# Sixteen quads of weight blocks by Strassen's seven products in a two-layer encoder on one core

## The reference

```python
h = rms_norm(x, norm_w[0]); z = h @ w_in_ab        # 4096 x 13312
y = concat([oa, ob]) * silu(gate); x = x + y @ w_out_ab   # 4096 x 4096
h = rms_norm(x, norm_w[1]); z = h @ w_in_c         # 4096 x 10240
x = x + (oc * silu(gate)) @ w_out_c                # 4096 x 4096
return rms_norm(x, final_norm_w)
```

## Time and profile before

| | |
|---|---|
| time, median of 3 runs | 2813.53 us (2813.2 to 2815.36) |
| profiled execution | 2814.37 us, of which the span of its instructions is 2812.6 us |
| PE busy | 2797.6 us, 99% |
| DVE busy | 1687.7 us, 60% |
| ACT busy | 1347.7 us, 48% |
| mean granted clock of PE | 0.998 of full speed |

### The profile page before, as it was taken

One profiled execution on the slowest core, in us unless ns is written; L12 is line 12 of the kernel. 1 busy time (PEld: TensorE's weight loads), 2 busy tenths in 40 slices (PEclk: granted clock), 3 DMA queues, 4 the chain that ended last, 5 costly groups with the idle time before them and its releaser, 6 DMA issues.

```text
span 2812.6 us, 37759 instructions
## 1 busy us (share of the span) xinstructions
PE 2797.6 (99%) x12681; PEld 2329.4 (83%) x12681; DVE 1687.7 (60%) x2103; ACT 1347.7 (48%) x1654; POOL 16.4 (1%) x14
## 2 busy tenths in 40 slices
PE   9999999999999999999999999999999999999998
PEld 7888888888888888888888888888888888888886
DVE  7766666556556555566665556666655666665554
ACT  6455455445444444444443445555544455543333
POOL 0000000000000000000000000000000000000000
PEclk9999999999999999999999999999999999999999
DMA  9777777777767777677777767777676777676665
GB/s 334 222 210 232 225 226 221 224 217 228 234 209 215 228 220 239 189 254 254 253 240 222 223 211 218 231 233 220 221 226 204 231 227 225 216 251 218 215 209 187
DMA packets 357923, 637.17 MB, mean 227 GB/s; under 512 B 25376, under 2 KB 79136, under 8 KB 357792
## 3 DMA queue, kind: packets, MB, share of 16 engines
q1 hardware_dynamic: 343824, 593.52, 67.7%
q10 hardware_dynamic: 13968, 41.95, 4.1%
HBM read 585.56 MB, written 49.81 MB: 226 GB/s over the span
## 4 chain that ended last, share of the span: by engine, by line
PE 99%; DMA 0%; issue 0%; DVE 0%; ACT 0%; POOLq 0%; POOL 0%; SPq 0%; DVEq 0%; ACTq 0%
PE proj L1098 32%; PE proj L1099 32%; PE proj L1100 32%; PE o_ps L1099 1%; PE o_ps L1098 1%; PE sc_ps L1100 1%; PE o_ps L1100 1%; PE sc_ps L1099 1%; PE sc_ps L1098 1%; DMA raw<-in_w_in_ab 0%; DVE w_lo L757 0%; DVE x_fin L1091 0%; ACT w_hi L637 0%; POOLq L268 0%; POOL rms L598 0%
## 5 line engine op out<-in xcount | busy, mean ns | idle before, releaser
L757 DVE TENSOR_TENSOR w_lo<-raw,w_hi 128x1024 fp32r<-128x1024 f32 x990 | 1208.5, 1221 | 856.7 <-ACT w_hi L637 850.5
L637 ACT ACTIVATE w_hi<-raw 128x1024 fp32r<-128x1024 f32 x990 | 1049.6, 1060 | 1148.6 <-PE proj L1100 1087.3
L1098 PE MATMUL proj<-w_hi,h_hi 128*128 128x512 f32 x2936 | 1143.4, 389 | 2.0 <-issue 1.5
L1099 PE MATMUL proj<-w_lo,h_hi 128*128 128x512 f32 x2936 | 1142.8, 389 | 0.0
L1100 PE MATMUL proj<-w_hi,h_lo 128*128 128x512 f32 x2936 | 1142.1, 389 | 0.0
L1100 PEld LDWEIGHTS proj<-w_hi,h_lo 128*128 128x128 f32 x2936 | 551.2, 188 | 114.9
L1098 PEld LDWEIGHTS proj<-w_hi,h_hi 128*128 128x128 f32 x2936 | 551.4, 188 | 114.5 <-issue 2.4
L1099 PEld LDWEIGHTS proj<-w_lo,h_hi 128*128 128x128 f32 x2936 | 551.4, 188 | 109.9
L1098 PE MATMUL proj<-w_hi,y_hi 128*128 128x512 f32 x1024 | 398.4, 389 | 0.0
L1099 PE MATMUL proj<-w_lo,y_hi 128*128 128x512 f32 x1024 | 398.4, 389 | 0.0
L1100 PE MATMUL proj<-w_hi,y_lo 128*128 128x512 f32 x1024 | 398.3, 389 | 0.0
(11 more groups left out here) (115 smaller groups left out, 975.5 us busy)
## 6 DMA issues: line engine op xcount, KB each, us to landing
raw<-in_w_in_ab SPq DMA_DIRECT2D x414, 512.0 KB, 4.4
raw<-in_w_in_c SPq DMA_DIRECT2D x320, 512.0 KB, 4.4
raw<-in_w_out_ab SPq DMA_DIRECT2D x128, 512.0 KB, 4.5
raw<-in_w_out_c SPq DMA_DIRECT2D x128, 512.0 KB, 4.5
head_turn<-head_stage SPq DMA_DIRECT2D x256, 96.0 KB, 1.9
head_land<-head_turn ACTq DMA_DIRECT2D x64, 384.0 KB, 5.5
landing<-group_turn ACTq DMA_DIRECT2D x31, 512.0 KB, 5.5
group_turn<-q_stage SPq DMA_DIRECT2D x64, 128.0 KB, 3.2
```

What stands on the lines that cost most here:

```text
L637: nc.scalar.activation(w_hi[:, slot], raw[:, slot], ACT.Copy).then_inc(hi_ready, 1)
L757: nc.vector.tensor_tensor(w_lo[:, slot], raw[:, slot], w_hi[:, slot].bitcast(F32), ALU.subtract) \
L1098: nc.tensor.matmul(dst, hi, r_hi, start=start, stop=False)
L1099: nc.tensor.matmul(dst, hi, r_lo, start=False, stop=False)
```

## The change

A *quad* is four blocks, two of each group: `B11` and `B12` (row tiles of chunk c1, groups 0 and 1), `B21` and `B22` (chunk c2). With the four 128-token by 256-row pieces of the activations `A11`, `A12` (token tile 0), `A21`, `A22` (token tile 1) it is a 2 x 2 product. The change computes it, for 16 quads, by seven products in place of eight (Winograd's form of Strassen's): seven products of six matmuls each in place of four blocks of twelve. Eleven pairs have quads: 6, 8, 10, 14, 16 and 28 one each (at block 9 in 6, 8 and 10, else at block 11), 15, 18, 23 and 29 two each (at blocks 4 and 13), and 30 two (at 2 and 11).

For each quad DVE makes four combinations of raw weights, `mix` (B12-B11), `mix3` (B22-B12), B22-mix and B21-that, each 128 x 1024; ACT rounds seven operands in place of four and DVE subtracts seven times in place of four. Operands 0, 2, 4, 6 use the ring's four slots, and operands 1, 3, 5 two spare slots that lie in tiles that are free then. The combinations of the activations (`make_sums`, S1 to S4, split once) are made in pairs 6, 14, 17 and 28, and reused by later pairs. Three products gather in PSUM banks of their own (`m1`, `m6` and `m7`, which is the bank of `o_ps`), and after the last quad of a pair seven additions of 128 x 512 (`fold`) bring them into `proj`. Pairs with quads take all of group 0 first, so group 0 ends at block 18 or 20 (30 in the last pair), where before in x1 and x2 pairs it ended at 30. Where such pairs stood in loops of two or three rounds these are written out, except for pairs 7 to 10. The diff, cut to what follows it:

```diff
+def with_quads(first, second, end=()):
+    blocks, quads = [], {}
+    for e in first:
+        if isinstance(e, tuple):
+            c1, c2 = e
+            quads[len(blocks)] = e
+            blocks += [(0, c1), (1, c1), (1, c2), (0, c2)]
+        else:
+            blocks.append((0, e))
+    return blocks + [(1, c) for c in second] + list(end), quads
+REST1, REST2 = [0, 1, *range(4, KC // 2)], [0, 1, *range(6, KC // 2)]
+VG_QUADS = with_quads([*REST1[:9], (2, 3), *REST1[9:]], REST1)
+X1_QUADS = with_quads([*REST1[:11], (2, 3), *REST1[11:]], REST1)
+TWO_QUADS = with_quads([*REST2[:4], (2, 3), *REST2[4:9], (4, 5), *REST2[9:]], REST2)
+LAST_QUADS = with_quads([*REST2[:2], (2, 3), *REST2[2:7], (4, 5), *REST2[7:-2]], REST2[:-2],
+                        [(g, EARLY + c) for g in range(2) for c in range(LATE)])
 
 
 XT_PIECES = ((0, 1), (1, 2)) + tuple((k, k + 2) for k in range(2, KC, 2))
...
-        (3, [Pair("in_ab", qk(1), "qk", "B", "vg", batch=4), Pair("in_ab", vg(1), "vg", "qk", "qk", v=2)]),
+        (1, [Pair("in_ab", vg(0), "vg", "qk", "qk", v=1, quads=VG_QUADS, heads=16, combine=((5, "vg", 0, 2),))]),
+        (2, [Pair("in_ab", qk(1), "qk", "B", "vg", batch=4),
+             Pair("in_ab", vg(1), "vg", "qk", "qk", v=2, quads=VG_QUADS, heads=20, heads_step=4)]),
+        (1, [Pair("in_ab", qk(3), "qk", "B", "vg", batch=6)]),
+        (1, [Pair("in_ab", vg(3), "vg", "qk", "qk", v=4)]),
         (1, [Pair("out_ab", out_cols(0), "x1", "B", "vg", batch=7)]),
...
-        (1, [Pair("in_c", kvc(0), "kv", "h", "x1", x_batch=3)]),
-        (1, [Pair("in_c", c(0), "qg", "k", "kv", v=5)]),
+        (1, [Pair("out_ab", out_cols(1), "x1", "h", "x1", x_batch=0, quads=X1_QUADS, heads=32,
+                  combine=((6, "x1", 0, 2), (26, "x1", 1, 4)))]),
+        (1, [Pair("out_ab", out_cols(2), "x1", "h", "x1", x_batch=1, quads=TWO_QUADS, heads=32)]),
+        (1, [Pair("out_ab", out_cols(3), "x1", "h", "x1", x_batch=2, quads=X1_QUADS, heads=32, spare="x1_end")]),
+        (1, [Pair("in_c", kvc(0), "kv", "h", "x1", x_batch=3, combine=((15, "qg", 0, 2), (19, "qg", 1, 4)))]),
+        (1, [Pair("in_c", c(0), "qg", "k", "kv", v=5, quads=TWO_QUADS, heads=32)]),
         (3, [Pair("in_c", c(1), "qg", "C", "qg", batch=8)]),
         (1, [Pair("in_c", kvc(1), "kv", "C", "qg", batch=11)]),
-        (1, [Pair("in_c", c(4), "qg", "k", "kv", v=6)]),
+        (1, [Pair("in_c", c(4), "qg", "k", "kv", v=6, quads=TWO_QUADS, heads=48)]),
...
-        (1, [Pair("out_c", out_cols(3), "x2", "none", "x2")]),
+        (1, [Pair("out_c", out_cols(1), "x2", "none", "x2", quads=X1_QUADS, heads=64,
+                  combine=((6, "x2", 0, 2), (26, "x2", 1, 4)))]),
+        (1, [Pair("out_c", out_cols(2), "x2", "none", "x2", quads=TWO_QUADS, heads=64)]),
+        (1, [Pair("out_c", out_cols(3), "x2", "none", "x2", quads=LAST_QUADS, heads=64)]),
     ]
-    n = x = second = 0
...
-                    if isinstance(p.n, int) and p.n * NB + b < RING:
-                        pass
-                    else:
-                        sp.wait_ge(lo_ready, p.n * NB + b - RING + 1)
+                    if b >= RING and p.quad_at(b - RING) is not None and p.quad_at(b - RING)[2] < 3:
+                        k, _, part = p.quad_at(b - RING)
+                        sp.wait_ge(mixed, QUAD * (p.quad_n + k) + part + 1)
...
+            def quad_hi(p, k, start, part):
+                n = p.o + p.op[start]
+                (mix, mix3), mixes_done = mix_of[p.out], QUAD * (p.quad_n + k)
+                b11, _, b22, b21 = (raw[:, (start + r) % RING] for r in range(QUAD))
+                earlier = p.o + p.op[list(p.quads)[k - 1]] if k > 0 else None
...
+                def hi(r, source, count=1):
+                    if r % 2 == 0:
+                        act.wait_ge(block_done, slot_free_after(p, start + r // 2))
+                    elif r == 5:
+                        act.wait_ge(block_done, n + 2)
+                    elif earlier is not None:
+                        act.wait_ge(block_done, earlier + (6 if r == 1 else 4))
+                    elif r == 1:
+                        act.wait_ge(block_done, p.o)
+                        act.wait_ge(folded, p.folds)
...
+                if part == 0:
+                    raw_landed(p, start)
+                    hi(0, b11)
+                if part == 1:
+                    raw_landed(p, start + 2)
+                    hi(1, b22)
+                if part == 2:
+                    act.wait_ge(mixed, mixes_done + 1)
+                    hi(2, mix[:])
+                    act.wait_ge(mixed, mixes_done + 2)
+                    hi(3, mix3[:])
+                if part == 3:
+                    raw_landed(p, start + 3)
+                    hi(4, b21)
+                    act.wait_ge(mixed, mixes_done + 3)
+                    hi(5, mix[:])
+                    act.wait_ge(mixed, mixes_done + 4)
+                    hi(6, b21, 2)
+            def copy_m1(p, b):
+                if p.quads and b == p.last_quad + QUAD:
+                    act.wait_ge(folded, p.folds)
+                    act.wait_ge(block_done, p.o + p.op[p.last_quad] + OPS)
+                    nc.scalar.activation(folds_of(p)[0], m1[:], ACT.Copy).then_inc(m1_copied, 1)
...
+            def quad_lo(p, k, start, part):
+                n = p.o + p.op[start]
...
+                b11, b12, b22, b21 = (raw[:, (start + r) % RING] for r in range(QUAD))
+                minus = lambda dst, a, b: nc.vector.tensor_tensor(dst, a, b, ALU.subtract)
...
+                def lo(r, source, count=1):
+                    hi, dst = weights_of(p, start, r)
+                    dve.wait_ge(hi_ready, n + r + 1)
+                    minus(dst, source, hi.bitcast(F32)).then_inc(lo_ready, count)
+                if part == 0:
+                    lo(0, b11)
+                if part == 1:
+                    second = (start + 1) % RING
+                    dve.wait_ge(raw_loaded[second], 16 * (p.n * (NB // RING) + (start + 1) // RING + (second > 1)))
+                    dve.wait_ge(lo_ready, n + 1)
+                    minus(mix, b12, b11).then_inc(mixed, 1)
+                    lo(1, b22)
+                if part == 2:
+                    dve.wait_ge(mixed, mixes_done + 1)
+                    minus(mix3, b22, b12).then_inc(mixed, 1)
+                    lo(2, mix)
+                    dve.wait_ge(mixed, mixes_done + 2)
+                    dve.wait_ge(lo_ready, n + 3)
+                    minus(mix, b22, mix).then_inc(mixed, 1)
+                    lo(3, mix3)
+                if part == 3:
+                    lo(4, b21)
+                    dve.wait_ge(mixed, mixes_done + 3)
+                    dve.wait_ge(lo_ready, n + 5)
+                    minus(b21, b21, mix).then_inc(mixed, 1)
+                    lo(5, mix)
+                    dve.wait_ge(mixed, mixes_done + 4)
+                    lo(6, b21, 2)
+                    dve.wait_ge(lo_ready, n + OPS)
...
+                    hi, lo = sums_of[stage][quad]
+                    if b == at + 1:
+                        dve.wait_ge(sums_hi, p.combined + k + 1)
+                        nc.vector.tensor_tensor(lo[:], sums, hi[:].bitcast(F32), ALU.subtract).then_inc(sums_split, 1)
+                        continue
+                    rows = slice(2 * c1, 2 * c1 + 4)
+                    a_hi, a_lo = (y_hi, y_lo) if p.w in ("out_ab", "out_c") else (h_hi, h_lo)
+                    dve.wait_ge(block_done, p.o)
...
+                    a11, a12 = parts[:, 0:2, 0:P], parts[:, 2:4, 0:P]
+                    a21, a22 = parts[:, 0:2, P:SEQ], parts[:, 2:4, P:SEQ]
+                    s1, s2, s3, s4 = (sums[:, r] for r in range(4))
+                    dve.wait_ge(sums_made, done + 1)
+                    nc.vector.tensor_tensor(s3, a11, a21, ALU.subtract)
+                    nc.vector.tensor_tensor(s1, a21, a22, ALU.add).then_inc(sums_made, 1)
+                    dve.wait_ge(sums_made, done + 2)
+                    nc.vector.tensor_tensor(s2, s1, a11, ALU.subtract).then_inc(sums_made, 1)
+                    dve.wait_ge(sums_made, done + 3)
+                    nc.vector.tensor_tensor(s4, a12, s2, ALU.subtract).then_inc(sums_made, 1)
...
+                    dve.wait_ge(m1_copied, p.pair_w + 1)
+                    dve.wait_ge(block_done, p.o + p.op[p.last_quad] + OPS)
+                    add(f2, m6[:], f1)
+                    dve.wait_ge(folded, p.folds + 1)
+                    add(f3, m7[:], f2)
+                if b == p.last_quad + QUAD + 2:
+                    dve.wait_ge(folded, p.folds + 2)
+                    add(f2, x22, f2)
+                    dve.wait_ge(folded, p.folds + 3)
+                    add(x22, x22, f3)
+                    add(x12, x12, f2)
+                if b == p.second_at:
+                    dve.wait_ge(block_done, p.o + p.op[p.second_at])
+                    add(x11, x11, f1)
+                    add(x21, x21, f3)
+                    dve.wait_ge(folded, p.folds + FOLDS)
 
...
```

(23 more changed lines are left out.)

255 lines of the change are left out of this document (209 added, 46 removed).

## The result

The changed kernel takes 2821.3 us in the median (2816.3 to 2824.5, 11 runs), the kernel before 2813.8 on the same chip (2813.0 to 2815.4, 11 runs): a ratio of 1.0025, 95% interval 1.0017 to 1.0034. It is 7.5 us slower where I had forecast 7 us faster.

What follows compares the result with a forecast made beforehand. PE was taken as the bound, busy 2797.6 of 2812.6 us. Products save 21.8 us, waits cost 14.7, so 7.1 us faster: 2807.3 from the profiled 2814.4, less 0.9 for the median, 2806.5 us; range 2795 to 2814.

Steps and rivals of the forecast that it cites:

- the folds cost nothing: On DVE, seven fold steps of about 0.7 us over four blocks; the ring's 5.7 us of lead hides them from PE.
- The waits in the quads: PE waits for late operands in quads with other DVE work in or ahead of them: 14.7 us with restarts.
- Pair 15: First quad waits at operands 3, 4, 5 (3.9 us), block 11 1.2, second quad 1.1: 6.2 us in all.
- The quads that I had put near their limit or below it: Pairs 8, 10, 16, 18 and 23: from 0.4 us in hand to 0.5 short at operand 5; 0.8 for all five.
- the forecast's own sign: If a quad in pair 28 and second quads in 18, 23, 29, 30 wait too, the DVE step was too small.
- a reserve of 1.5 us: In a quad in quiet surroundings DVE's operands come at least 1.5 us before PE wants them, so it costs nothing.
- DVE's steps: Eleven DVE steps a quad, 1.26 us after a result just made, otherwise 1.17: 13.2 us against PE's 9.5.
- the rival with 1.35 us for every step: All ten DVE steps at 1.35 us, a quad 1.5 us longer: waits of 32 us, 2824 us; chance 0.13.
- The saving: On PE, 42 matmuls a quad in place of 48, 1.36 us each quad, 21.8 us for 16 quads.
- the rival of products that bring nothing: On PE, seven products cost as much as eight because matmuls go at a longer step: 2828 us; chance 0.02.
- that of the clock: PE's clock falls in the waits, nine slow matmuls in each of seven quads: 13 us, 2819 us; chance 0.03.
- The added work: DVE's busy time grows by 137 us and more than 30 for sums and folds, ACT's by 51.

Runs made afterwards that it cites:

- experiment 1: Changed kernel with DVE's fold steps put ahead of the subtraction of their block instead of behind it: 2809.7 us, ratio 0.9983 to the kernel before.
- experiment 3: Changed kernel with one quad instead of two in pairs 15, 18, 23, 29 and 30, eleven quads, folds as in the change: 2815.1 us.
- experiment 5: Changed kernel with folds ahead of the subtraction and one quad in each of the eleven pairs: 2803.3 us, ratio 0.9959 to the kernel before.
- experiment 6: experiment 1 with the landed turn behind the block's rounding and subtraction on ACT and DVE, in all pairs with quads: 2807.3 us.
- experiment 9: experiment 5 and experiment 6 together: folds first, one quad a pair, landed turn behind the subtraction in all pairs with quads: 2802.8 us.
- experiment 10: experiment 9 with the landed turn behind the subtraction only in pairs 6, 8 and 10: 2800.3 us, ratio 0.9951 to the kernel before.
- experiment 12: experiment 10 with two quads again in pairs 18, 23 and 29, fourteen quads: 2799.8 us, ratio 0.9947 to the kernel before.
- experiment 11: Changed kernel with the quads of pairs 14, 16 and 28 at block 9 instead of 11, folds left behind the subtraction: 2823.0 us.
- experiment 7: experiment 6 with the last pair's first quad at block 3 instead of 2: 2805.7 us, ratio 0.9969 to the kernel before.
- experiment 2: Changed kernel with all folds left out, so three products don't reach the output: 2807.8 us, ratio 0.9977 to the kernel before.
- experiment 8: experiment 1 with two of each quad's four raw-weight combinations (mix, mix3) on POOL instead of DVE: 2831.7 us, ratio 1.0063 to the kernel before.

## Why the prediction was wrong, by its own steps

**The step that failed** is that the folds cost nothing because "the 5.7 us of lead cover them". I counted the seven steps at 0.7 us each, which is what they take (0.69), and set them against the lead of the ring. But the lead is that of a subtraction. The folds stand behind the subtraction for a block that PE wants one block later than the folds' result: even in quiet surroundings that subtraction is ready 2.4 us after PE starts block 16, the three steps take 2.0 more, and PE starts block 18 at 5.4. That is 1.0 us in hand, not 5.7, and after a quad DVE is late. A single walk of DVE's list from the quad to the second group, as I did for the quads, would have shown it. It is 11.6 us; experiment 1 took it away by order alone (11.7). With it the sum would have been 2818, inside what was measured.

**The waits in the quads** were sized at 14.7 us and are 18.0 (19.3 measured directly, as said above). The place was right where I walked the list: pair 6 waits at operands 2, 3 and 5 as said (3.1 us, forecast 3.9), the first quad of pair 30 at 2, 3 and 5 (2.7, forecast 2.85), pair 14 at 5 (0.8, forecast 1.0). Pair 15 waits at 4 and 5 in its first quad, not at 3, not at block 11, and at 3 and 5 in its second: 4.5 us, forecast 6.2. The quads that I had put near their limit or below it were too cheap: pairs 8, 10, 16, 18 and 23 cost 5.0 us (forecast 0.8), all of it in 10, 18 and 23, pair 29's and 30's second quads 2.0 (forecast nothing). By the forecast's own sign, waits in such quads would mean a slower step on DVE; that wasn't it (below). In pair 18 it was the time at which the load for operand 1 lands. ACT and then DVE in their timelines (operands 0 and 1, and the landed keys):

```profile
1630.21 1.06 ACT L812 ACTIVATE w_hi<-raw 128x1024 fp32r<-128x1024 f32 x1 [0.53 <-PE proj L1414]
...
1634.84 1.06 ACT L812 ACTIVATE spare_c_hi<-raw 128x1024 fp32r<-128x1024 f32 x1 [3.57 <-DMA raw<-in_w_in_c]
```

```profile
1631.37 1.23 DVE L984 TENSOR_TENSOR w_lo<-raw,w_hi 128x1024 fp32r<-128x1024 f32 x1 [0.43 <-ACT w_hi L812]
...
1635.93 1.23 DVE L984 TENSOR_TENSOR spare_c_lo<-raw,spare_c_hi 128x1024 fp32r<-128x1024 f32 x1 [2.00 <-ACT spare_c_hi L812]
...
1641.81 1.22 DVE L1286 TENSOR_TENSOR kT_lo<-landing,kT_hi 128x1024 fp32r<-128x1024 f32 x1
```

From low 0 to low 1 it is 4.56 us, not 2.33; PE started the quad at 1638.1, so the block landed 3.3 us ahead of it, not 6.5. SP issued that load at 1628.74, 9.4 us ahead of the quad and not 11.0: the subtraction that frees its slot ended at 1627.97, and four transfers of the turn (L626) kept SP until 1628.70. And it landed 6.1 us after its issue, not 4.5. The landing alone would use up a reserve of 1.5 us; here the landed keys, 1.13 us just ahead of low 4, come on top. In pair 23 they stand in the first quad too, and PE waits at operands 4 and 5 there as well; the second quads of both pairs, without them, have no wait. In the second quad of pair 29 the distance from low 0 to low 1 is 3.8 us, also behind a landing. Why pair 10 waits (0.17 and 0.58 us) stays open: in the trace of experiment 1 it doesn't, and pair 8 does.

**DVE's steps** were right. In pair 6 the quad, with the landed turn in it, is

```profile
573.97 1.22 DVE L984 TENSOR_TENSOR w_lo<-raw,w_hi 128x1024 fp32r<-128x1024 f32 x1
...
577.58 1.22 DVE L1286 TENSOR_TENSOR kT_lo<-landing,kT_hi 128x1024 fp32r<-128x1024 f32 x1
578.71 1.22 DVE L984 TENSOR_TENSOR zb<-raw 128x1024 f32<-128x1024 f32 x1
579.85 1.22 DVE L984 TENSOR_TENSOR w_lo<-za,w_hi 128x1024 fp32r<-128x1024 f32 x1
581.17 1.23 DVE L984 TENSOR_TENSOR za<-raw,za 128x1024 f32<-128x1024 f32 x1
...
587.27 1.23 DVE L984 TENSOR_TENSOR w_lo<-raw,w_hi 128x1024 fp32r<-128x1024 f32 x1
```

14.5 us less the turn's 1.1: 13.4, forecast 13.2; the rival with 1.35 us for every step would have 14.7. That rival had the time nearly right (2824) by a mechanism that isn't there. A step that doesn't wait for the one before it follows after 1.14 us (578.71 to 579.85), one that does after 1.32 (579.85 to 581.17). The Trainium skill's rule that the semaphore costs nothing extra (VectorE: DVE Perf Modes, "The DRAIN you can't avoid") differs from these rows by 0.18 us; the measurement decides.

**The saving** of 21.8 us is right: the quads without a wait take 9.52 us. All waits at the prices above, products and order account for the change and for experiments 1, 3, 5, 6, 9, 10 and 12 to within 1 us of the spans traced. For experiment 10: 2.5 us of waits less 11 x 1.36 = 15.0, and 1.6 for the order, is 14.1 us faster; the medians differ by 13.9, the spans by 14.7. The same account leaves 1.2 and 1.3 us open in experiments 11 and 7, 1.9 in 2 and 3.8 in 8. So the rival of products that bring nothing falls, and so does that of the clock: the granted clock was 0.999 in the mean.

**The added work**: DVE's busy time grew by 206 us; 137 are the combinations and the further subtractions of the quads, 11 x 7 x 0.69 = 53 the folds, the rest the sums. ACT's grew by 59, forecast 51, without the sums and copies.

## What to carry to other kernels

A lead protects a step only by the distance between its place in the engine's list and the moment at which its result is wanted; what stands ahead of it in the list, with its own waits, is taken off. So for each added step ask what stands ahead of it that is wanted later, and put the step that is wanted sooner first: here that alone was worth 11.7 us. And where a feeding engine is slower than the fed one for a stretch, price a rare gain for each place by its own waits: in the changed kernel one quad in place of two in five pairs, at later blocks, was 6.2 us faster with five products more to do.

## What the runs showed of the hardware

In experiment 8 a DVE step with two inputs in SBUF and a step of POOL didn't make headway beside each other. DVE's subtraction that began in POOL's step took 2.55 us and ended 1.08 us after it, and POOL's next, begun before that subtraction had ended, took 3.20 us where the one that began ahead of it took 2.40. Of the 24 subtractions of 128 x 1024 in that trace that start inside a POOL step, 23 end 1.07 to 1.10 us after it (the other began 0.02 us ahead of its end). The transposition, with one input, took 1.24 us beside POOL, as without it (1.25). The Trainium skill (SBUF — State Buffer, "SBUF: two separate sides") says that the two engines take a shared pair of ports as an exclusive lock for a whole instruction, DVE with two SBUF inputs among the cases. The trace agrees, by the 1.08 us behind POOL's end.

The changed kernel's times spread over 8 us (2816.3 to 2824.5), those before over 2.4 (over 2.6 to 3.7 beside the experiments) and those of experiments 9, 10 and 12, five runs each, over less than 2: with the lead used up, a shift in a landing seems to reach PE. That was not tested by itself.
